# Last two expert units summed on chip, earlier rows read back during them, final rows on VectorE alone

## The reference

```python
gates = p_grp * w_top                      # two weights for each token
gu = einsum('td,edf->tef', ht, w_gu[sl])   # gate and up, 256 wide each
act = silu(g_act) * up * combine
out = out + einsum('tef,efd->td', act, w_dn[sl])
...
x = x + moe(rmsnorm(x)); return rmsnorm(x) * norm_final
```

## Time and profile before

| | |
|---|---|
| time, median of 3 runs | 1193.43 us (1193.3 to 1196.03) |
| profiled execution: time, span | 1192.7, 1190.9 us |
| PE busy, DVE, ACT, POOL | 94%, 45%, 30%, 11% of the span |
| granted TensorE clock, mean | 0.982 |
| bytes read and written in HBM | 167.38 and 33.05 MB |

### The profile page before, as it was taken

One profiled execution on the slowest core, in us unless ns is written; L12 is line 12 of the kernel. 1 busy time (PEld: TensorE's weight loads), 2 busy tenths in 40 slices (PEclk: granted clock), 3 DMA queues, 4 the chain that ended last, 5 costly groups with the idle time before them and its releaser, 6 DMA issues.

```text
span 1190.9 us, 16483 instructions
## 1 busy us (share of the span) xinstructions
PE 1116.9 (94%) x6487; PEld 615.0 (52%) x6487; DVE 537.8 (45%) x1196; ACT 351.6 (30%) x676; POOL 131.5 (11%) x154
## 2 busy tenths in 40 slices
PE   6999999999999899897799999999999999997886
PEld 6545744444844689775474444456643333332232
DVE  6876233334399544796572222335532121211116
ACT  4114631111676332204664100265301111100004
POOL 2000012220000000001100000132011111111004
PEclk9999999999999999999899999999999999999998
DMA  8111022131112452420114000462349999999958
GB/s 284 36 58 53 22 74 78 55 98 48 34 59 110 191 146 68 171 101 1 73 70 177 0 1 1 147 255 99 131 170 347 410 397 426 420 423 425 407 195 335
DMA packets 65973, 196.35 MB, mean 165 GB/s; under 512 B 24444, under 2 KB 41056, under 8 KB 55392
## 3 DMA queue, kind: packets, MB, share of 16 engines
q1 hardware_dynamic: 59184, 178.25, 39.4%
q0 software_dynamic: 6656, 16.95, 3.8%
q10 hardware_dynamic: 48, 0.01, 0.0%
HBM read 167.38 MB, written 33.05 MB: 168 GB/s over the span
## 4 chain that ended last, share of the span: by engine, by line
PE 75%; DVE 11%; issue 4%; ACT 3%; DMA 1%; POOL 0%; DVEq 0%; SPq 0%; POOLq 0%; ACTq 0%
PE bank L2643 20%; PE bank L1554 13%; PE bank L1610 8%; PE bank L1577 6%; PE bank L1672 2%; PE bank L1625 2%; PE bank L2770 2%; PE bank L1540 1%; PE bank L805 1%; PE bank L916 1%; PE bank L866 1%; PE bank L1692 1%; PE bank L853 1%; PE bank L884 1%; DVE arena L756 1%
## 5 line engine op out<-in xcount | busy, mean ns | idle before, releaser
L2643 PE MATMUL bank<-arena 128*128 128x512 f32 (+3 forms) x1032 | 357.4, 506 | 6.6 <-ACT arena L2147 5.4
L2643 PEld LDWEIGHTS bank<-arena 128*128 128x128 f32 x1032 | 196.4, 192 | 161.6 <-issue 140.7
L1554 PE MATMUL bank<-arena 128*32 128x512 f32 x1344 | 152.4, 606 | 14.6 <-issue 13.7
L1554 PEld LDWEIGHTS bank<-arena 128*32 128x32 f32 x1344 | 46.4, 112 | 116.7 <-issue 116.7
L1610 PE MATMUL bank<-arena 128*128 128x512 f32 x220 | 95.6, 592 | 0.0
L1327 DVE TENSOR_TENSOR arena<-arena,bank 128x256 f32<-128x256 f32 x21 | 8.9, 422 | 158.3 <-ACT arena L1213 122.6
L1577 PE MATMUL bank<-arena 128*32 128x512 f32 x672 | 76.5, 595 | 2.4 <-ACT arena L1217 1.4
L2147 ACT ACTIVATE arena<-bank 128x512 f32<-128x512 f32 (+1 forms) x57 | 28.5, 505 | 164.4 <-PE bank L2643 163.9
L1370 DVE TENSOR_TENSOR arena<-arena,bank 128x512 f32<-128x512 f32 x32 | 22.0, 689 | 100.1 <-PE bank L1610 79.5
L1610 PEld LDWEIGHTS bank<-arena 128*128 128x128 f32 x220 | 41.3, 190 | 49.7 <-issue 49.7
L1213 ACT ACTIVATE arena<-bank 128x256 f32<-128x256 f32 x21 | 8.1, 384 | 165.7 <-PE bank L1554 165.7
(11 more groups left out here) (411 smaller groups left out, 1585.8 us busy)
## 6 DMA issues: line engine op xcount, KB each, us to landing
arena<-in_w_e_gu SPq DMA_DIRECT2D x26, 2048.0 KB, 14.3
arena<-in_w_e_dn SPq DMA_DIRECT2D x32, 1024.0 KB, 15.0
arena<-in_w_in SPq DMA_DIRECT2D x11, 1024.0 KB, 5.2
arena<-y_d SPq DMA_DIRECT2D x8, 1024.0 KB, 11.1
arena<-hz_d SPq DMA_DIRECT2D x4, 1792.0 KB, 8.9
arena<-in_w_e_gu SPq DMA_DIRECT2D x6, 1024.0 KB, 13.1
arena<-in_w_e_gu SPq DMA_DIRECT2D x12, 512.0 KB, 14.3
pk_d<-arena SPq DMA_DIRECT2D x8, 640.0 KB, 2.9
```

The costliest lines, as they stand in the source:

```text
L1554: ins = mm(bank[part, :], hgT[:, k, part], w_gu(es[i] % NB, k), start=(k == 0), stop=(k == KT - 1))
L2643: ins = mm(psum[PROJ_BANKS[u % 3]][0:rows, 0:n], lhs(k), rhs(k), start=(k == 0), stop=(k == kt - 1))
```

## The change

1. **Late units.** The results of units 19 and 20 (LATE = 2) are not scattered. Their tokens are treated as two more tiles, NT and NT + 1: GpSimd gathers their x2 rows (from a new DRAM copy, x2_d) and the row of y_d of their other expert, and PE adds the results from ysb by products with small matrices of weights (`pe_late`), made during units 3 to 9 (`late_indices`, `late_tokens`, `late_equal`, `late_counts`, `late_sums`, `late_weights`).
2. **Read-back.** SP reads tiles 0 to 7 of y_d when the scatters of units 17 and 18 have landed, behind its last expert load; y_d is zeroed early in the kernel (`clear_rows`, eight DMAs of 1 MB), since rows of late units are not written.
3. **Final rows.** PE and GpSimd no longer take part: VectorE makes each sum in two steps and scales in one (`dve_rows`), ScalarE squares and takes the root (`act_rows`). Tiles 0 and 1 are summed beside unit 20; ScalarE's first square stands ahead of its copy of unit 20. Then comes a written order of 10 tiles. SP stores tiles 0 to 4; GpSimd stores the late tiles and tiles 5 to 7 with indirect DMAs, by indices that leave out rows held elsewhere, and the late tiles wait until SP's five have landed.
4. **Order.** `overflow` comes behind the final rows. The gains are loaded before the expert stage, and each x2 tile is stored behind its xn store.

```diff
@@ sp_tail, act_experts, dve_experts
+                sp.wait_ge(s["t_m_e"], 2 * (m + 1))
+                sp.dma_start(x2_d[m * P:(m + 1) * P, :], x2[:, m]).then_inc(s["t_x2"], 16)
...
+            sp.wait_ge(s["t_r_dve"], 6)
+            sp.dma_start(w_d.rearrange("(m p k) o -> p m (k o)", p=P, k=TK), w_mk).then_inc(s["t_xn"], 16)
+            sp.wait_ge(s["t_x2"], X2_STORED)
+            sp.dma_start(fin_g, a["norm_final"].unsqueeze(0).to_broadcast([P, D])).then_inc(s["t_x2"], 16)
             sp_experts(sp, moe, 0)
+            sp_rows(sp, 0)
             with overflow(sp):
...
-            sp_tail3(sp)
+                sp_rows(sp, 1)
...
+                    if isinstance(p, int):
+                        for step in ACT_BESIDE.get(u, ()):
+                            act_rows(act, 0, *step)
                     act.wait_ge(q["dn"], UN * p + u)
...
+        ORDER = ((0, 1, 2, 3, NT, 4, NT + 1, 5, 6, 7), tuple(range(NT)))
+        ACT_BESIDE = {UN: [("square", 0)]}
+        POOL_STEPS = ([("store", i) for i in (NT, NT + 1) + BY_POOL], [])
+        DVE_BESIDE = {UN - 1: [("sum", 0), ("sum", 1)]}
+        DVE_AFTER = ([("scale", 0), ("sum", 2), ("other", NT), ("other", NT + 1), ("scale", 1), ("sum", 3),
+                      ("scale", 2), ("sum", NT), ("scale", 3), ("sum", 4), ("scale", NT), ("sum", NT + 1),
+                      ("scale", 4), ("sum", 5), ("scale", NT + 1), ("sum", 6), ("scale", 5), ("sum", 7),
+                      ("scale", 6), ("scale", 7)],
...
+        def late_weights(pool, last_y):
+            pool.wait_ge(s["t_xn"], 16 * (NT + 1))
+            pool.wait_ge(s["t_m_mx"], NT + 1)
+            for l in range(LATE):
+                at = slice(late_u[l], late_u[l] + 1)
+                for to, index in ((w_own, ix_sc[:, at]), (w_ot, ix_ot[:, l:l + 1])):
+                    pool.indirect_dma_start(to[:, l:l + 1], None, w_d, bass.IndirectOffsetOnAxis(ap=index, axis=0),
+                                            bounds_check=last_y, oob_is_err=False).then_inc(s["l_w"], 16)
+        def pool_late(pool, q, last_row, last_y):
...
+            pool.wait_ge(q["gu"], UN - 1)
+            for l in range(LATE):
+                at = slice(late_u[l], late_u[l] + 1)
+                pool.indirect_dma_start(xr[l], None, x2_d, bass.IndirectOffsetOnAxis(ap=ix_ga[:, at], axis=0),
+                                        bounds_check=last_row, oob_is_err=False).then_inc(s["l_w"], 16)
+            pool.wait_ge(s["l_w"], L_W + 48 * LATE)
...
+            for l in range(LATE):
+                pool.indirect_dma_start(yo[l], None, y_d, bass.IndirectOffsetOnAxis(ap=ix_ot[:, l:l + 1], axis=0),
+                                        bounds_check=last_y, oob_is_err=False).then_inc(s["l_w"], 16)
+        def act_rows(act, r, what, i):
...
+            act.wait_ge(s["f_c"], j + 1)
+            act.wait_ge(s["xs_r"], G4 + j - 3)
+            nc.scalar.activation(row_sq, sum_of(i), ACT.Square, accum_out=ss[:, c]).then_inc(s["t_q_e"], 1)
+            act.wait_ge(s["t_q_e"], CT * NHALF + j + 1)
+            nc.scalar.activation(rms[:, c], ss[:, c], ACT.Sqrt, bias=epsc[:, 0:1],
+                                 scale=1.0 / D).then_inc(s["rms_r"], 1)
+        def dve_rows(dve, v, link, r, what, i):
+            if what == "sum" and i in LATE_ROWS:
...
+                    ins = v.tensor_tensor(xr[l][:, cols], xr[l][:, cols], psum[6 * l + hf][:, :], ALU.add)
+            elif what == "sum":
+                y_wait(dve, i, r)
+                link(v.scalar_tensor_tensor(yg[i][:, 0], yg[i][:, 0], wts[:, 0, i:i + 1], x2[:, i], ALU.mult,
+                                            ALU.add))
+                v.scalar_tensor_tensor(yg[i][:, 0], yg[i][:, 1], wts[:, 1, i:i + 1], yg[i][:, 0], ALU.mult,
+                                       ALU.add).then_inc(s["f_c"], 1)
+            elif what == "other":
+                l = LATE_ROWS.index(i)
+                dve.wait_ge(s["l_w"], L_W + 64 * LATE)
+                link(v.scalar_tensor_tensor(xr[l], yo[l], w_ot[:, l:l + 1], xr[l], ALU.mult, ALU.add))
+            else:
...
+                link(v.reciprocal(rms[:, c], rms[:, c]))
+                v.scalar_tensor_tensor(row_out(i), sum_of(i), rms[:, c], fin_g, ALU.mult,
+                                       ALU.mult).then_inc(s["xs_r"], 1)
+        def sp_rows(sp, r):
             for m in range(NT):
+                if r == 0 and m == 0:
+                    sp.wait_ge(moe["dn"], UN - LATE)
+                    for i in range(2):
+                        sp.wait_ge((moe["st0"], moe["st1"])[(UN - LATE - 1 - i) % 2], rows_of(UN - LATE - 1 - i))
+                if r == 0 and m == 3:
+                    sp.wait_ge(moe["gu"], UN - 1)
+                if r == 0 and m == 6:
+                    sp.wait_ge(moe["dn"], UN - 1)
                 if m >= 4:
+                    y_wait(sp, m - 4, r)
                 sp.dma_start(yg[m], y_d[m * TK * P:(m + 1) * TK * P, :].rearrange("(p k) d -> p k d", k=TK)).then_inc(
                     Y_IN[m % 4][0], 16)
+            for m in BY_SP if r == 0 else range(NT):
+                sp.wait_ge(s["xs_r"], G4 + place_of(r, m) + 1)
+                sp.dma_start(out[m * P:(m + 1) * P, :], yg[m][:, 1]).then_inc(s["f_ot"], 16)
+            sp.wait_ge(s["f_ot"], 16 * (3 + len(BY_SP) + r * NT))
+            sp.wait_ge(s["l_w"], L_OUT + 16 * (LATE + len(BY_POOL)))
```

More of the change, by code:

```diff
@@ L1305, in act_tail2 @@
             act_experts(act, moe, 0)
+            for step in ACT_AFTER[0]:
+                act_rows(act, 0, *step)
             with overflow(act):
@@ L1310, in act_tail2, with dve_experts @@
                     pass_end(act, moe, p + 1)
-            act_tail3(act, link, stats)
-        def dve_experts(dve, v, q, p):
+                for step in ACT_AFTER[1]:
+                    act_rows(act, 1, *step)
+        def dve_experts(dve, v, q, p, link=None):
             def tokens(u):
@@ L1530, in dve_tail2 @@
                     pass_end(dve, moe, p + 1)
-            dve_tail3(dve, v, link, inverse_rms)
+                for step in DVE_AFTER[1]:
+                    dve_rows(dve, v, link, 1, *step)
         def pe_experts(pe, mm, q, p):
@@ L1590, in pe_experts @@
                     down(u - 1)
+                if u == 4 and isinstance(p, int):
+                    late_tokens(pe, mm)
+                if u == 7 and isinstance(p, int):
+                    late_counts(pe, mm)
         def rows_of_blocks(pe, mm):
@@ L1778, in pe_tail2 @@
             pe_experts(pe, mm, moe, 0)
+            pe_late(pe, mm)
             with overflow(pe):
@@ L1863, in pool_tail2 @@
             pool_experts(pool, moe, 0, last_row, last_y)
+            pool_late(pool, moe, last_row, last_y)
+            for step in POOL_STEPS[0]:
+                pool_rows(pool, 0, last_row, *step)
             with overflow(pool):
+                pool.wait_ge(s["l_w"], L_OUT + 16 * (LATE + len(BY_POOL)))
+                for u in late_u:
+                    scatter(pool, moe, u, last_y)
                 pass_end(pool, moe, 0)
@@ L1957, in sp_tail3 @@
[L1957 to L1960 removed]
+        BY_POOL = (5, 6, 7)
+        BY_SP = tuple(m for m in range(NT) if m not in BY_POOL)
+        LATE_ROWS = (NT, NT + 1)
+        ORDER = ((0, 1, 2, 3, NT, 4, NT + 1, 5, 6, 7), tuple(range(NT)))
+        L_W = 16 * 4 * CT
+        L_OUT = L_W + 64 * LATE
+        ACT_BESIDE = {UN: [("square", 0)]}
@@ new lines, in hybrid_trunk @@
+        ACT_AFTER = ([("square", i) for i in ORDER[0][1:]], [("square", i) for i in ORDER[1]])
+        POOL_STEPS = ([("store", i) for i in (NT, NT + 1) + BY_POOL], [])
[4 more added lines that the diff above has]
+                      ("scale", 6), ("scale", 7)],
+                     [("sum", 0)] + [st for i in range(1, NT) for st in (("sum", i), ("scale", i - 1))]
+                     + [("scale", NT - 1)])
@@ new lines, in pe_late @@
+        def pe_late(pe, mm):
+            pe.wait_ge(moe["y"], 2 * UN)
+            pe.wait_ge(s["t_m_rc"], NT + 1)
+            for l in range(LATE):
+                for hf in range(2):
+                    for of in range(LATE):
+                        ins = mm(psum[6 * l + hf][:, :], lt_S[:, of, l], ysb[late_u[of] % 2][:, hf * HALF:(hf + 1) * HALF],
+                                 start=(of == 0), stop=(of == LATE - 1))
+                ins.then_inc(s["f_p"], 1)
+        def act_rows(act, r, what, i):
+            j = place_of(r, i)
+            c = slice((G4 + j) % 4, (G4 + j) % 4 + 1)
+            act.wait_ge(s["f_c"], j + 1)
[4 more added lines that the diff above has]
+                                 scale=1.0 / D).then_inc(s["rms_r"], 1)
```

230 lines of the change are left out of this document (138 added, 92 removed).

## The result

| | us |
|---|---|
| before, median of 8 runs beside it | 1193.87 (1190.69 to 1196.71) |
| after, median of 8 runs | 1200.93 (1198.68 to 1204.86) |
| ratio, 95% interval | 1.0062 (1.0042 to 1.0082) |
| the profiled execution of after | 1203.07, its span 1200.9 |

The kernel became slower by 0.6%, 7 us by the medians; I had forecast 1195.9 and a range up to 1200. The sign was on the side that I gave 0.36.

A forecast was written before the change was run, and what follows sets the result against it. DMA bounds the last units, then VectorE's work sets the end. VectorE's end 1184.5, landing 1188.6, plus 0.55, 3.05 and 0.4 gives 1192.6; 0.8 elsewhere makes span 1193.4, profiled 1195.2, median 1195.9 us; range 1191 to 1200.

The forecast's parts named there:

- the side that I gave 0.36: The chance given to a slower kernel: 0.18 for the jump, 0.15 for late data, 0.03 from the summed case's upper tail.
- Unit 20 "+0.5 late": Expert stage: 0.3 us for the four gathers of single weights and 0.2 for PE's small late-tile products.
- VectorE "starts at 1144.15": After unit 19: tile 0's read lands at 1144.15 as VectorE finishes unit 19's copy at 1144.13; neither waits.
- 28 steps: VectorE's full-row steps in the final rows: 1.28 us each, plus 0.04 gap if linked, less 0.08 overlap if not.
- "Other ... Issued by about 1143 ... they are there at 1152": Late tiles' y_d gathers: landed at 1152, wanted at 1153.7, 1.5 us of cover; 0.3 added.
- slower by data: Rival: tile 0's read or the gathers for other come late, up to 6 us, priced at 4: 1199.9; chance 0.15.
- After VectorE: Kernel end: last store landing 4.1 us after issue, overflow test 0.55, jump 3.05, then 0.4 to the span's end.
- the second rival, a free jump: Kernel end: the jump over the skipped overflow body is near or prefetched, 0.04 to 0.2 instead of 3.05: 1193.0; chance 0.15.
- pe_late: PE's eight products for the late tiles: 0.45 us each, ready by 1153.9, hidden.
- Added elsewhere: Work outside the final path: zeroing y_d, x2 stores, gains and weights cost nothing; gathers and small products included, 0.8 us.
- the slower jump: Rival at the kernel's end: the jump costs SP its own 6.5 us again: 1199.3; chance 0.18.
- the faster steps: Rival in the final rows: VectorE's steps take 1.00 us, 28 steps saving 6.7: 1189.2; chance 0.12.

The follow-up runs named there:

- late_work_shifted: The changed kernel with the late tiles' index steps and PE products moved from units 3 to 9 to units 14 to 19; ratio 1.0053 against the kernel before.
- warm_before_20: The changed kernel with three unused products filling PE's wait before unit 20's gate-up; ratio 1.0068 against the kernel before.
- start_free: The changed kernel with late-tile steps at units 14 to 19, four fill products in unit 20's bank, y_d gathers not waiting for x2's; ratio 1.0067 against before.
- best_version: The changed kernel with PE's first step for tiles 4 to 7, late-tile steps at units 14 to 19, three fill products, other asked later; ratio 0.9997 against before.
- others_asked_later: The changed kernel with VectorE's two steps other placed behind sum 3 and scaling 2; ratio 1.0055 against the kernel before.

## Why the prediction was wrong, by its own steps

The sum ended at +2.5 over the span before; measured from S1 it was +6.3. The 3.8 are:

- **Unit 20 "+0.5 late"** was 1.8 (1.3 of error). The 0.3 for the gathers is neither shown nor refuted. The step that failed is "at most eight products of under 0.45, some 0.7 in all; as the DMA is what the last units wait for, 0.2": the products took 2.3, and at units 4 to 8 PE had no slack either. The rows said so, PE busy 12.00 of 12.00 at 948 and at 1032. I read the DMA column of these rows and not the first. late_work_shifted showed it; by all profiles together the shift is worth 1.2 at unit 19 and not 1.8, the rest is spread between executions.
- **The duration of unit 20's gate-up** had no term at all (1.7). I took 7.1 from the earlier trace rows and let it only start later. The lower clock behind the wait added 1.7, as warm_before_20 showed. Why the profile of before did not pay it at unit 20 stays open: there unit 19 had the low clock, with no cost.
- **VectorE "starts at 1144.15"** falls with these two: the first sum came straight after unit 19's copy, at 1151.25. The read of tile 0, issued after 8.7 and not 9.0, did not decide in this run, but did as soon as the copy came earlier (start_free, best_version).
- **28 steps**: right. 1.28 each (the 2.52 of a scaling beside GpSimd's multiplications, L1922 in the earlier trace rows, is 1.28 at L2107, where GpSimd multiplies nothing), no overlap beyond the 0.08 that I had read; from the first sum to VectorE's end I had 40.35, and it took 41.83 (1151.25 to 1193.08), of which 1.48 are the wait of the next step.
- **"Other ... Issued by about 1143 ... they are there at 1152"** failed (1.2 after the 0.3 that I had added for it). The gathers of y_d wait for those of x2, 12.7 after the issue of the second (1136.97), so they went out at 1149.65 and 1150.95 and took 11.4. The code has that wait (`L_W + 48 * LATE`); I had costed the landing of a gather and not the one queued in front of it. It was my rival "slower by data", at the place it named, but with 1.5 and not 4. In other profiles of the same order the wait was 0.3 to 3.0, so the 1.5 is one draw.
- **After VectorE** (8.1 predicted, 7.8 measured): right in size, incomplete in cause. The last landing came 3.6 after its issue for 4.1, the test 0.5 for 0.55, the jump 2.7 for 3.05; the quiet value was the right choice over 6.5. But GpSimd's DRAIN ends 0.5 later than SP, and the second rival, a free jump, would not have gained its 3 us even if true.
- **pe_late** was costed at 0.45 a product and took 0.89 (7.13 for eight): I had read a record as a product, and a product of 128x512 leaves two. It stayed hidden.
- **Added elsewhere**: zeroing y_d and the stores of x2 cost nothing that shows. SP's issue at 164.66 came at 164.98, and its last issue of a gate-up load ahead of unit 0 moved from 868.03 to 868.55. The weights and gains at 877, put at nothing, stay open: ahead of S1 the two profiles differ by 2.8 from unit 0's first gather on, outside the 3.8 of this list.

1.3 + 1.7 + 1.2 are 4.2, less 0.4 by smaller terms (the tail 0.3 of it). The medians differ by 7.1, 0.8 more than the 6.3 from S1. The time outside the span is 0.3 of it (1.8 before, some 2.1 after, by time and span of each run); the rest is within the spread of the runs, and small against the 3.7 that the two profiles differ ahead of S1. Some of the fit is therefore luck: the four pieces compare two single executions. Neither the slower jump nor the faster steps among my rivals occurred.

## What to carry to other kernels

Before a few small products are put into another engine's stream at a price of nothing, read that engine's busy column in the very window where they go: in a stretch where two resources are both full, each delays the end. When a block of products on the last path stands behind a wait, price it at the slower clock too (here 1.7 us for 7.1), and look which of the blocks in a profile has it: one further ahead can have it for nothing. And where an end has several queues behind the last result, sum each to its own end: removing the longest shows nothing while another is as long.

## What the runs showed of the hardware that I had not expected

- GpSimd's DRAIN at the end of the block lasted until 6.7 to 7.4 us after the start of its last indirect DMA (1183.00 to 1189.7, 1190.97 to 1197.9, 1193.37 to 1200.7). That the indirect DMA is the reason is not shown. In the kernel before, the last indirect DMA stands at 1149.24 and the last multiplication ends at 1182.99, and the DRAIN, hidden there behind SP, lasts until 1188.0:

```profile
L38 POOLq DRAIN  x1: 8320/8320/8320, 1179.7 to 1179.7; - x1
```

  The Trainium skill ("VectorE: DVE Perf Modes", The DRAIN you can't avoid) gives the DRAINs that the runtime puts around a kernel a constant 12 ns or so on all five engines. Those measured here stand on a line of the kernel (L38), so the figure may not be meant for them; on SP they took 7 to 63 ns, on GpSimd 5697 to 8320.
- The wait ahead of a gate-up does not forecast its clock alone: 2.28 us were followed by 7.1 in the profile of before, and 2.29 by 8.77 in others_asked_later. Both stood behind a unit 19 of 8.78. What makes the difference stays open.

```profile
1136.24 8.77 PE L1601 MATMUL bank<-arena 128*32 128x512 f32 x64 [2.29 <-issue]
```
